# One layer norm of a transformer kernel from sums of z and of its squares, and two products that begin with two output tiles together

## The reference

```
def conformer_conv(h, w_pw1, b_pw1, w_dw, b_dw, ln_g, ln_b, w_pw2, b_pw2):
    a, gt = jnp.split(h @ w_pw1 + b_pw1, 2, axis=-1)
    z = a * jax.nn.sigmoid(gt)
    z = lax.conv_general_dilated(
        z, w_dw[:, None, :], window_strides=(1,), padding=[(CONV_WIDTH - 1, 0)],
        dimension_numbers=('NWC', 'WIO', 'NWC'), feature_group_count=D_MODEL) + b_dw
    z = jax.nn.silu(layernorm(z, ln_g, ln_b))
    return z @ w_pw2 + b_pw2
...
x = x + swiglu(rmsnorm_2(x, ffn_norm[0]), ...)      # FFN of layer 0
x = x + conformer_conv(rmsnorm_2(x, mix_norm[1]), ...)
x = x + swiglu(rmsnorm_2(x, ffn_norm[1]), ...)      # FFN of layer 1
```

## Time and profile before

| | |
|---|---|
| median of 3 runs | 3101.41 us (3096.34 to 3102.07) |
| profiled execution | 3101.02 us, span 3099.3 us from its first to its last instruction |
| mean granted TensorE clock | 0.964 |
| TensorE matmul busy | 2939.4 us, 95% |
| VectorE busy | 2017.2 us, 65% |
| ScalarE busy | 1152.4 us, 37% |
| GpSimd busy | 74.9 us, 2% |
| pw1 with the VectorE part of the convolution beside it | about 2070 to 2251 us |
| TensorE's part of the convolution | 2251 to 2309 us |
| layer norm | 2309 to 2359 us |
| pw2 | 2343 to 2426 us |

### The profile page before, as it was taken

One profiled execution on the slowest core, in us unless ns is written; L12 is line 12 of the kernel. 1 busy time (PEld: TensorE's weight loads), 2 busy tenths in 40 slices (PEclk: granted clock), 3 DMA queues, 4 the chain that ended last, 5 costly groups with the idle time before them and its releaser, 6 DMA issues.

```text
span 3099.3 us, 39335 instructions
## 1 busy us (share of the span) xinstructions
PE 2939.4 (95%) x15355; PEld 2363.3 (76%) x15355; DVE 2017.2 (65%) x3446; ACT 1152.4 (37%) x1949; POOL 74.9 (2%) x147
## 2 busy tenths in 40 slices
PE   3999999999998999899999999989988999999999
PEld 3868875565787888777888888868857788888887
DVE  5444215557535455648777778778995787777785
ACT  3234225542322555534333334441125433333444
POOL 1000000110004000000000000000000000000000
PEclk7999999999998999799999999999998999999999
DMA  8010210012210000033333356321102233334633
GB/s 310 21 31 21 62 27 18 18 55 69 82 31 8 1 1 1 28 109 102 109 109 109 109 197 214 94 63 52 38 10 68 95 123 109 109 109 164 229 101 102
DMA packets 180755, 256.26 MB, mean 83 GB/s; under 512 B 29367, under 2 KB 131675, under 8 KB 176219
## 3 DMA queue, kind: packets, MB, share of 16 engines
q1 hardware_dynamic: 176432, 228.25, 22.5%
q10 hardware_dynamic: 4139, 25.50, 2.0%
HBM read 186.62 MB, written 67.11 MB: 82 GB/s over the span
## 4 chain that ended last, share of the span: by engine, by line
PE 85%; DVE 9%; ACT 2%; issue 1%; DMA 0%; DVEq 0%; ACTq 0%
PE ps L1511 26%; PE ps L1519 14%; PE ps L1466 10%; PE ps L1414 4%; PE ps L1070 3%; PE ps L1083 3%; PE ps L1325 3%; PE ps L1107 3%; PE ps L949 2%; PE ps L1237 2%; PE ps L1217 2%; PE ps L1262 2%; PE ps L1396 2%; PE ps L1378 2%; PE ps L1575 2%
## 5 line engine op out<-in xcount | busy, mean ns | idle before, releaser
L1511 PE MATMUL ps<-x_ops,w_ring 128*128 128x512 f32 x3696 | 840.4, 390 | 6.2 <-DVE even_rows L2886 3.1
L1511 PEld LDWEIGHTS ps<-x_ops,w_ring 128*128 128x128 f32 x3696 | 693.5, 188 | 151.1 <-issue 7.8
L1519 PE MATMUL ps<-a_ring,w_ring 128*128 128x512 f32 x1848 | 419.5, 389 | 0.0
L1519 PEld LDWEIGHTS ps<-a_ring,w_ring 128*128 128x128 f32 x1848 | 347.0, 188 | 72.2 <-DVE w_ring L2827 0.5
L1466 PE MATMUL ps<-h_high,ring_parts 128*128 128x512 f32 x1024 | 320.3, 395 | 18.0 <-DVE h_low L2338 9.3
L2056 ACT ACTIVATE w_ring<-ring 128x512 fp32r<-128x512 f32 x230 | 144.2, 629 | 300.6 <-PE ps L1511 284.8
L1466 PEld LDWEIGHTS ps<-h_high,ring_parts 128*128 128x128 f32 x1024 | 193.6, 190 | 63.7 <-issue 13.5
L2347 DVE TENSOR_TENSOR ring_parts<-ring,ring_parts 128x1024 fp32r<-128x1024 f32 (+1 forms) x65 | 77.2, 1188 | 203.9 <-ACT ring_parts L1713 203.5
L1466 PE MATMUL ps<-h_low,ring_parts 128*128 128x512 f32 x512 | 200.9, 392 | 0.0
L2827 DVE TENSOR_TENSOR w_ring<-ring,w_ring 128x512 fp32r<-128x512 f32 x230 | 157.5, 685 | 38.8 <-ACT w_ring L2056 38.8
L2069 ACT ACTIVATE a_ring<-a_raw 128x512 fp32r<-128x512 f32 x150 | 94.6, 631 | 206.6 <-PE ps L1519 177.1
(11 more groups left out here) (458 smaller groups left out, 4703.9 us busy)
## 6 DMA issues: line engine op xcount, KB each, us to landing
a_raw<-act_kept SPq DMA_DIRECT2D x70, 512.0 KB, 3.8
act_kept<-even_rows SPq DMA_DIRECT2D x12, 1536.0 KB, 5.1
act_kept<-odd_rows SPq DMA_DIRECT2D x10, 1536.0 KB, 5.1
ring<-in_ffn_w_gate_dram SPq DMA_DIRECT2D x12, 1024.0 KB, 5.9
ring<-in_ffn_w_up_dram SPq DMA_DIRECT2D x12, 1024.0 KB, 6.1
ring<-in_conv_w_pw_dram SPq DMA_DIRECT2D x24, 512.0 KB, 3.8
late<-in_ffn_w_gate_dram SPq DMA_DIRECT2D x10, 1024.0 KB, 5.9
late<-in_ffn_w_up_dram SPq DMA_DIRECT2D x10, 1024.0 KB, 6.1
```

Source lines behind the costliest of these rows:

```text
L1511: last = mm(o, w_ring[:, i % 4, wp_, P * k:P * k + P], x_ops[:, X_OP[p], rp_, k, :], start=p in "176" and k == 0 and p_ == 0, stop=k == 3 ...
L1519: last = mm(bank(OUT_BANK[DOWN_GROUP[p] + c_]), w_ring[:, (A_UNITS + b) % 4, wp_, P * c_:P * c_ + P], a_ring[:, b % 4, rp_, :], start=p in ...
```

## The change

It does four things. The first two weight tiles of pw1 are split before the FFN's last half squares, no longer after the barrier. Both pw1 and pw2 begin with two tiles together: for each input chunk the matmuls of both tiles are issued (`first_two`), and both end with the last chunk. The layer norm's statistics come from sums of z and of z squared: ScalarE squares the uncentred chunks as they are ready, GpSimd adds chunks 1, 2, 3, 5 and 6 of z and of the squares in ten additions, VectorE squares and adds its last own chunk (4), TensorE makes column sums of both, and VectorE forms mean, variance and its clamp at zero in five instructions of 128x8. And pw2's first weight splits move: ScalarE's into the convolution, VectorE's ahead of the mean. The matmuls of the mean now write banks 4 and 5.

More of the change, by code:

```diff
@@ L235, in build @@
         sum_taps = part(22144, (N_EVEN, KC))
+        z_sum = flat_ht[:, 0:S]
+        z_squares = lambda k: part(S * k, (S,))
+        z_stats = [stat[:, 2 * i:2 * i + 2, :].rearrange("p a b -> p (a b)") for i in range(2)]
         s = Signals()
@@ L1561, in _ @@
             stage(pe, "x_3")
-            for n in range(KC):
+            for f_sem in (s.gate_free, s.up_free):
+                pe.wait_ge(f_sem, N_PW + 1)
+            first_two(T_PW1, s.h_ok, H_OK[4], (s.gate_out, s.up_out))
+            for n in range(1, KC):
                 for kind in range(2):
@@ L1596, in _, with columns @@
                 tap_sums(c_, 0)
[L1597 to L1601, removed]
+                if c_ < len(PE_CONV) - 1:
+                    fold(c_, 1)
+                    fold(c_, 0)
+            def columns(at, tile, done=None):
+                for t in range(TB):
+                    last = mm(ps[:, 3072 + at + t:3073 + at + t], tile(t), ones[:, 0:1],
+                              start=at + t == 0 and done is None, stop=done is not None, skip_group_check=True)
+                if done is not None:
+                    last.then_inc(done, 1)
@@ L1688, in square, with root @@
                 f(sc[:, k % 2, :], src[:, k, :], ACT.Square).then_inc(s.sq_ready, 1)
[L1690 to L1696, removed]
+            def root(n):
+                a.wait_ge(s.sum_done, n - (n > 5))
+                f(root_sum, ps[:, 3072:3072 + TB], ACT.Sqrt, bias=EPS, scale=1.0 / D).then_inc(s.rs_ready, 1)
             a.wait_ge(s.x_in, 32)
@@ L2206, in _, with chunk_square @@
                     high(T_PW1 + 2 * n + 3)
+            planes = lambda row: row.rearrange("p (two m) -> p two m", two=2)
+            a.wait_ge(s.up_out, N_PW + KC)
+            def chunk_square(k):
+                f(planes(z_squares(k)), zc[:, k], ACT.Square).then_inc(s.sq_ready, 1)
+            for k in range(3):
+                a.wait_ge(s.zc_ok, k + 1)
+                chunk_square(k)
             for c_, n in enumerate(PE_CONV):
@@ L2218, in _ @@
                       bias=cols[:, V_BDW + n:V_BDW + n + 1]).then_inc(s.zc_ok_pe, 1)
[L2219 to L2227, removed]
+                    if n == KC - 1:
+                        a.wait_ge(s.zc_ok_pe, 2 * c_ + turn + 1)
+                        f(z_squares(n)[:, 512 * parity:512 * parity + 512], zc[:, n, parity, :], ACT.Square).then_inc(s.sq_ready, 1)
+                if c_ == 0:
[5 more added lines that the diff above has]
+                    high(T_PW2 + c_)
+            a.wait_ge(s.zc_sum, 3)
+            f(root_sum, z_stats[1], ACT.Sqrt, bias=LN_EPS).then_inc(s.rs_ready, 1)
             for k in range(KC):
@@ L3155, in ffn @@
                         half_squares(l, b - 68)
+                if l == 0:
+                    low(T_PW1)
+                    low(T_PW1 + 1)
                 for c_ in range(5):
@@ L3242, in _ @@
             planes = lambda row: row.rearrange("p (two m) -> p two m", two=2)
[L3243 to L3263, removed]
+            last_own = KC - 4
@@ L3264, in _, with centred @@
+            v.wait_ge(s.zc_ok, last_own + 1)
+            tt(planes(z_squares(last_own)), zc[:, last_own], zc[:, last_own], mul).then_inc(s.sq_used, 8)
[4 more added lines that the diff above has]
+            tt(z_squares(0), z_squares(0), z_squares(last_own), add).then_inc(s.zc_sum, 1)
             low(T_PW2)
             low(T_PW2 + 1)
-            root(5)
+            def centred(k):
+                stt(zc[:, k], planes(bank(4, 2)), -1.0 / D, zc[:, k], mul, add).then_inc(s.xc_done, 1)
```

22 lines of the change are left out of this document (7 added, 15 removed).

## The result

The changed kernel takes 3112.0 us (median of 5 runs, 3109.0 to 3115.3), the kernel before beside it 3097.45 (5 runs): ratio 1.0042, 95% interval 1.0031 to 1.0052. A second comparison (6 and 13 runs) gave 1.0032, 1.0020 to 1.0043. Predicted were 3111 and +10.2 us; the two comparisons say +13 and +10 by their ratios (the medians of the first lie 14.5 apart).

A forecast was written before the change was run, and what follows sets the result against it. TensorE, busy 95% of the span, bounds the kernel, so only its idle or low-clock stretches can give; -4.6 (pw1) + 20.7 (held steps) - 5.9 (layer norm and pw2's pair) = +10.2 on 3101, predicted 3111 us, range 3098 to 3117.

The forecast's parts named there:

- pw1: Start of pw1: early weight split and two tiles together let the third tile start 4.6 us earlier, bounds 3.5 and 5.5.
- Held steps: Convolution: GpSimd's ten additions hold VectorE's steps, 0.4 us for the first, 2.25 each for nine; +20.7, bounds 16.2 and 21.1.
- The open assumption: Convolution: the step's form, SCALAR_TENSOR_TENSOR, which no profile row shows held, was taken to behave like TENSOR_TENSOR.
- without holding: Rival, convolution: the steps' form doesn't compete with GpSimd, so no delay; 3083 us (3079 to 3087), chance 0.13.
- without a turn for GpSimd: Rival, convolution: GpSimd waits while VectorE's steps follow closely, eight additions come after them; 3109 us, chance 0.12.
- the rival of cheap additions: Rival, convolution: additions cost 1.8 us each, 16.2 instead of 20.7, and the clock rises early; 3105 us, chance 0.18.
- The first addition: Convolution: GpSimd's first addition lies beside VectorE's last gating, which reads PSUM, so it costs only 0.4 us.
- The break-even of 1.2 us a hold: Convolution: the change gains as long as each addition holds VectorE for less than about 1.2 us.
- Layer norm and pw2's pair: From VectorE's last convolution step to pw2's third tile: new statistics and two tiles together save 5.9 us net of low clock.
- the sign named for full clock in these sums: Layer norm: if the column sums run at 2.4 GHz, this term is some 5 to 8 us better.

The follow-up runs named there:

- The early table: Changed kernel with a one-column sigmoid on ScalarE right behind its last split of pw1's normed rows, so its table loads early; ratio to before 1.0021.
- the additions alone: Kernel before plus only GpSimd's ten additions, into two rows nobody reads; pw2's first matmul 18.3 us late, ratio to before 1.0051.
- half-length additions: Changed kernel with nine of GpSimd's ten additions over 512 columns instead of 1024; ratio to before 0.9997.
- TensorE kept busy: Changed kernel with 21 useless matmuls of 512 columns on TensorE while it waits for z's sum; ratio to before 1.0022.
- no additions: Changed kernel with GpSimd's ten additions left out, so the sums lack five chunks; ratio to before 0.9970.
- the fastest kernel: Changed kernel with sums on VectorE instead of GpSimd, mean before column sums, early sigmoid, and pw2's bank-freeing copy ahead of the split; ratio to before 0.9954.
- the fastest kernel without its two small edits: Changed kernel with sums on VectorE and mean before column sums, but no early sigmoid and no bank-freeing copy ahead of pw2's split; ratio to before 0.9969.

## Why the prediction was right, point by point

The sign, the mechanism and nearly the sum held. By S, M and T:

**pw1: predicted -4.6, measured -3.1.** The step up to the third tile was right: both first tiles ended at 2091.6 (forecast 2091.9), the stall was 2.2 (2.15), the third tile started at 2093.85 (2094.05). What was missing is the clock behind that stall, 1.7 us. The early table gives both back. The end of pw1, by GpSimd's release, is S + 187.8, against S + 190.8 in the run of the additions alone.

**Held steps: predicted +20.7, measured +17.6.** The open assumption, that SCALAR_TENSOR_TENSOR is held like TENSOR_TENSOR, is shown by the additions alone. The rivals without holding and without a turn for GpSimd are out: it got one behind each single step. Mis-sized was the price of one: 1.96 us, not 2.25. I had taken 2.37 from L3370 in the earlier trace rows as the form of the new additions, but that line is a subtraction of two tensors. It is no wait that makes it long: one of its rows starts at 992.45 and takes 2.40 while VectorE does nothing but one instruction that reads PSUM (the kernel before):

```profile
992.45 2.40 POOL L3370 TENSOR_TENSOR big<-ht,big 128x1024 f32<-128x1024 f32 x1
```

An addition takes 2.00, an accumulating one 2.06 where it waits least, and that is what VectorE waits for. By price the rival of cheap additions (1.8) was nearer than the forecast; its clock, which rises early, did not come. The first addition, which I put at 0.4, was free. Nine held it is. The break-even of 1.2 us a hold comes out too: at 1.96 the change costs 8.2 us, at 0.89 (half-length additions) it gains 1.7, which puts it at about 1.1, an estimate on a straight line between the two.

**Layer norm and pw2's pair: predicted -5.9, measured -6.4.** From VectorE's last step to M: 33.6 us, forecast 33.9. From M to T: 26.15, forecast 26.3. Inside, the first columns took 3.57 (3.55), the fold 1.86 (2.1), the mean 6.3 (5.8), the last columns 4.2 (4.4). But the reason given, a clock that is low because TensorE idled, is only part of it: kept busy, it saved 3.1 us, where the sign named for full clock in these sums was 5 to 8.

**Sum: predicted +10.2, measured 8.2 by the traces**, 10 and 13 by the two comparisons. The forecast of 3111 lies 1 us from the median of the first. Part of that is luck: -4.6 was too good by 1.5 and +20.7 too bad by 3.1, and the forecast set out from 3101 where the kernel before took 3097.45 beside the changed one. Two figures of the prediction do not follow from its own terms, and neither is part of the sum: nine times 2.25 are 20.3 and not 19.8, and in the rival without holding the multiplications begin near 2321 and not 2322, which would make it 3082. What the 2 to 5 us between traces and comparisons are isn't settled; no row behind T shows them.

The Trainium skill (SBUF — State Buffer, Who interferes with whom) has the rule for the held steps, and says that who issues first decides who blocks. The trace agrees: steps of 0.74 take 2.86, additions of 2.00 take 2.71. By the figure in its GPSIMD Engine Reference (Performance versus the Vector engine) I had estimated 2.25 us for an addition of 1024; the trace has 2.00 alone.

## What to carry to other kernels

Work moved to an idle engine is not free if it shares what the busy engine reads through: here a VectorE instruction on SBUF tensors waits out each whole GpSimd instruction, so an addition that VectorE makes in 1.24 us costs it 1.96 when it is given away. Compare those two numbers before the move, and give GpSimd only stretches where VectorE reads PSUM or idles. When two tiles are begun together, look at what used to lie behind the first: the bare piece costs its own length and, at 2.2 us here, the clock besides.

## What the runs showed of the hardware that was not expected

- TensorE can lose its clock while busy. Column sums (128x128 by 128x1) began at 2.4 GHz and ended at 1.2 in three traces (no additions; TensorE kept busy; the fastest kernel), with no wait over 1.2 us ahead of them and once behind 18 us of dense matmuls. In a fourth, the fastest kernel without its two small edits, 32 such instructions behind the same mean ran at 1.00 to the end. DMA doesn't decide it: its share in the windows where the clock fell was 0.90, 0.03 and 0.00. What does is open. The mean, dense matmuls, ran at 1.00 in both kernels that put it first.
- A stall of 2.2 us at the start of pw1 was followed, not at once but during the next matmuls, by some 3 us at 1.2 GHz; stalls of 1.2 and 1.3 us never were (five). Behind pw2's pair a stall of 2.3 us was followed by a low clock in four traces and not in five others.
- Where both have work queued, VectorE and GpSimd take turns, one instruction each, though VectorE's take 0.7 us and GpSimd's 2.0.
- A TENSOR_SCALAR with one SBUF tensor in float32 is held as well: 2.49 us instead of 0.55.
